# Two hybrid mixers: the pre-norm's token scale moved behind the first units, two norms merged into one stage, and filler matmuls dropped at the merged norms

## The reference, cut to what matters

```python
def second_block(x, ...):                    # x is _rmsnorm(h, final_norm) of the first block
    for l in range(DEPTH):                   # DEPTH = 2
        h = rms_norm(x, norm_mix_pre[l])
        mix = hybrid_mixer(h, w_in[l], ...)  # h @ w_in, h @ w_gate, four branches, w_out
        x = x + rms_norm(mix, norm_mix_post[l])
        h = rms_norm(x, norm_ffn_pre[l])
        x = x + rms_norm(swiglu(h, w_ffn_in[l], w_ffn_out[l]), norm_ffn_post[l])
    return x
```

## Time and profile before

| | us |
|---|---|
| median of 3 runs (lowest to highest) | 3116.38 (3113.12 to 3118.59) |
| the profiled execution, its own time | 3116.57 |
| its span in the profile | 3114.8 |
| PE busy | 3023.1 (97%) |
| PE weight loads busy | 2644.7 (85%) |
| DVE busy | 1688.2 (54%) |
| ACT busy | 1341.7 (43%) |

### The profile page before, as it was taken

The page is one execution under the profiler, slowest core; times in us unless marked ns, Lnnn a source line. Parts: engine busy times, 40 slices in busy tenths (PEclk is TensorE's granted clock), DMA queues, the critical chain, the costliest instruction groups (busy, mean ns, idle before and its releaser), DMA issues.

```text
span 3114.8 us, 52232 instructions
## 1 busy us (share of the span) xinstructions
PE 3023.1 (97%) x20192; PEld 2644.7 (85%) x20192; DVE 1688.2 (54%) x2641; ACT 1341.7 (43%) x1953; POOL 0.2 (0%) x4
## 2 busy tenths in 40 slices
PE   6999999989999999999998999999999999999999
PEld 4777778877777878888888999999899999998998
DVE  4333354545333353334666566677766666776666
ACT  3322233424322343323335655555654545556544
POOL 0000000000000000000000000000000000000000
PEclk9999999999999999999999998999999999999999
DMA  8656453115566233332322655455456544554564
GB/s 266 178 172 189 144 173 98 55 35 156 160 190 191 83 96 102 91 101 81 121 83 85 181 172 162 127 158 161 131 149 188 170 132 141 163 156 135 156 180 131
DMA packets 639022, 439.41 MB, mean 141 GB/s; under 512 B 22180, under 2 KB 627200, under 8 KB 638720
## 3 DMA queue, kind: packets, MB, share of 16 engines
q1 hardware_dynamic: 638848, 436.93, 47.5%
HBM read 430.84 MB, written 1.05 MB: 139 GB/s over the span
## 4 chain that ended last, share of the span: by engine, by line
PE 89%; DVE 7%; ACT 2%; issue 1%; DMA 1%; SPq 1%; ACTq 0%; DVEq 0%
PE ps L446 27%; PE ps L447 26%; PE ps L448 26%; PE ps L526 2%; DVE wlo L395 2%; PE ps L841 1%; ACT whi L389 1%; DVE normed L2326 1%; PE ps L1601 1%; PE ps L1569 1%; DVE xl L2318 1%; PE ps L1589 1%; DMA mod_w<-ada_w 0%; PE ps L868 0%; DVE h_gates L3043 0%
## 5 line engine op out<-in xcount | busy, mean ns | idle before, releaser
L446 PE MATMUL ps<-xh,whi 128*128 128x256 f32 (+1 forms) x3744 | 1221.7, 326 | 19.8 <-DVE wlo L395 5.2
L447 PE MATMUL ps<-xl,whi 128*128 128x256 f32 (+1 forms) x3744 | 1199.5, 320 | 0.0
L448 PE MATMUL ps<-xh,wlo 128*128 128x256 f32 (+1 forms) x3744 | 1198.5, 320 | 0.0
L395 DVE TENSOR_TENSOR wlo<-raw,whi 128x1024 fp32r<-128x1024 f32 x732 | 867.9, 1221 | 197.5 <-ACT whi L389 191.8
L389 ACT ACTIVATE whi<-raw 128x1024 fp32r<-128x1024 f32 x732 | 747.4, 1052 | 477.9 <-PE ps L448 432.5
L446 PEld LDWEIGHTS ps<-xh,whi 128*128 128x128 f32 x3744 | 715.7, 191 | 112.8 <-issue 32.8
L448 PEld LDWEIGHTS ps<-xh,wlo 128*128 128x128 f32 x3744 | 715.7, 191 | 51.3
L447 PEld LDWEIGHTS ps<-xl,whi 128*128 128x128 f32 x3744 | 716.5, 191 | 47.9
L446 PE MATMUL ps<-hid_h,whi 128*128 128x512 f32 (+1 forms) x1056 | 358.2, 339 | 0.2 <-DVE wlo L395 0.2
L447 PE MATMUL ps<-hid_l,whi 128*128 128x512 f32 (+1 forms) x1056 | 355.5, 337 | 0.0
L448 PE MATMUL ps<-hid_h,wlo 128*128 128x512 f32 (+1 forms) x1056 | 355.0, 336 | 0.0
(11 more groups left out here) (361 smaller groups left out, 2660.3 us busy)
## 6 DMA issues: line engine op xcount, KB each, us to landing
raw<-ffn_w_in SPq DMA_DIRECT2D x176, 512.0 KB, 4.8
mod_w<-ada_w SPq DMA_DIRECT2D x72, 1024.0 KB, 5.2
raw<-w_in SPq DMA_DIRECT2D x96, 512.0 KB, 4.5
raw<-w_ffn_in SPq DMA_DIRECT2D x88, 512.0 KB, 4.7
raw<-w_gate SPq DMA_DIRECT2D x64, 512.0 KB, 4.2
raw<-ffn_w_out SPq DMA_DIRECT2D x64, 384.0 KB, 4.0
raw<-ffn_w_out SPq DMA_DIRECT2D x64, 320.0 KB, 3.7
raw<-w_branch SPq DMA_DIRECT2D x32, 512.0 KB, 3.5
```

What stands on the lines that cost most here:

```text
L395: nc.vector.tensor_tensor(wlo[:, s, h, :], raw[:, s, h, :], whi[:, s, h, :].bitcast(F32), ALU.subtract).then_inc(S("lo_ready"), 1)
L446: nc.tensor.matmul(dst, w_h, x_h, start=start, stop=False)
L447: nc.tensor.matmul(dst, w_h, x_l, start=False, stop=False)
L448: return nc.tensor.matmul(dst, w_l, x_h, start=False, stop=stop)
```

## The change

The two norms in front of each mixer become one stage `merge`, as in front of the feed-forward networks. The mixer's first two units (`among_first`, `among_second`) take the one-column sums and the spread between their matmuls. All six units read unscaled chunks, and DVE multiplies by `tok_scale` where it empties their banks, in place of the copy. The other products of the mixer need scaled chunks: beside units 3 and 4, DVE and ACT make them in the second half of `xh`/`xl` (`second_pieces`, `second_highs`), and the small product and `beside_block` read them there. In layer 0 `merge` writes `hT` directly and adds nothing. At all four merged norms the two filler matmuls ahead of the spread and the three behind it are dropped. The last norm (`renorm` before `store`) keeps its form.

```diff
@@ pe_blocks @@
-                for j, b in sorted(order) if x_ready else order:
+                if x_ready:
+                    order.sort()
+                for j, b in order:
...
-                m.then_inc(S("mm_done"), 1)
+                    if (j, b) == order[-1]:
+                        m.then_inc(S("mm_done"), 1)
+                    if among:
+                        among(k, b)
@@ schedule @@
-        schedule += [("renorm", hT, lambda k: V("final_norm", k), True)]
+        post, by_post = lambda k: V("final_norm", k), False
...
-                ("norm", hT, 1, None, gain("norm_mix_pre_2")),
-                ("mamba", layer, w_in),
+                ("merge", hT if layer == 0 else h_out, post, gain("norm_mix_pre_2"), by_post),
+                ("mamba", layer, w_in, gain("norm_mix_pre_2")),
...
-                ("renorm", h_out, gain("norm_ffn_post_2"), layer == 0, True),
             ]
-        schedule += [("store",)]
+            post, by_post = gain("norm_ffn_post_2"), True
+        schedule += [("renorm", h_out, post, False, by_post), ("store",)]
@@ tensor: beside_block @@
-                        m = three(dst, w_h[:, k % 4, cols], w_l[:, k % 4, cols], xh[:, k, 0:T], xl[:, k, 0:T],
+                        m = three(dst, w_h[:, k % 4, cols], w_l[:, k % 4, cols], xh[:, k, T:2 * T], xl[:, k, T:2 * T],
@@ tensor: mamba @@
+                def among_first(k, b):
+
+                    if b == 1 and k:
+                        renormed_sum(k - 1)
+                    if (k, b) == (DC - 1, 1):
+                        renormed_sum(k)
+
+                def among_second(k, b):
+
+                    if (k, b) == (2, 0):
+                        spread_rstd(NT, 0)
+
+                pe.wait_ge(S("root_ready"), c.of["norm"])
@@ tensor: stages @@
                 elif stage == "merge":
-                    spread_rstd(NT)
+                    spread_rstd(NT, 0)
                     c.add(renorm=DC)
                     x_ready = norm_ready(1)
-                    warm(3, 3)
@@ scalar: mamba @@
-                pairs_of(act, c, 3, lambda i, s: None, ahead=past_odd(act_split, 1), first=True)
+                def second_highs(i, s):
+
+                    if (i, s) == (0, 0):
+                        token_scale()
+                    for k in range(4 * s, 4 * s + 4) if i == 1 else ():
+                        act.wait_ge(S("norm_prod"), c.of["norm_prod"] + k + 1)
+                        nc.scalar.activation(xh[:, k, T:2 * T], normed[:, k, 0:T], ACT.Copy).then_inc(S("norm_hi"), 1)
+                pairs_of(act, c, 3, second_highs, ahead=past_first(act_split), unroll=True)
@@ vector: merge @@
+                added = src is not hT
...
-                    if 1 <= k <= DC:
+                    if added and 1 <= k <= DC:
@@ vector: mamba @@
+                def second_pieces(k0):
+
+                    for k in range(k0, k0 + 4):
+                        nc.vector.scalar_tensor_tensor(out=normed[:, k, 0:T], in0=hT[:, k, 0:T], scalar=gain(k),
+                                                       in1=tok_scale, op0=ALU.mult, op1=ALU.mult).then_inc(S("norm_prod"), 1)
+                    for k in range(k0, k0 + 4):
+                        dve.wait_ge(S("norm_hi"), c.of["norm_hi"] + k + 1)
+                        nc.vector.tensor_tensor(xl[:, k, T:2 * T], normed[:, k, 0:T], xh[:, k, T:2 * T].bitcast(F32),
+                                                ALU.subtract).then_inc(S("norm_lo"), 1)
...
-                    fm_evac(m_in, 0, T)(dve, c, i, s)
-                pairs_of(dve, c, 3, evacuate, ahead=past_odd(dve_split, 1), unroll=True)
+                    if (i, s) == (0, 0):
+                        token_scale()
+                    if i == 1:
+                        second_pieces(4 * s)
+                    unit_done(dve, c, i, s)
+                    u = 2 * i + s
+                    nc.vector.tensor_tensor(m_in[:, 2 * u:2 * u + 2, :], ps[:, 2 * s:2 * s + 2, 0:T],
+                                            tok_scale.unsqueeze(1).to_broadcast([P, 2, T]), ALU.mult)\
+                        .then_inc(S("evac_done"), 1)
+                    if (i, s) == (0, 0):
+                        dve_split(dve, 0, 0, c.units + 2)
+                pairs_of(dve, c, 3, evacuate, ahead=past_first(dve_split), unroll=True)
```

More of the change, by code:

```diff
@@ L859, in ss_sum @@
                 m.then_inc(S("ss_mm"), 1)
[L861 to L871, removed]
             def renormed_sum(k):
@@ L1451, in mamba @@
                 beside = Beside(0, MAMBA_PLACES)
+                def among_first(k, b):
[7 more added lines that the diff above has]
+                pe.wait_ge(S("root_ready"), c.of["norm"])
                 pairs_of(pe, c, 3, lambda i, s: pe_blocks(pe, c, i, s, DC, T, xh, xl, 2, 256,
-                                                          x_ready if is_first(i, s) else None), first=True)
+                                                          x_ready if is_first(i, s) else None,
+                                                          (among_first, among_second)[s] if isinstance(i, int) and i == 0 else None),
+                         first=True)
+                norm_ready(1)(DC - 1)
                 pe.wait_ge(S("m_sw_lo"), layer + 1)
                 for t in range(NT):
-                    tt = slice(t * P, (t + 1) * P)
+                    tt = slice(T + t * P, T + (t + 1) * P)
                     for k in range(DC):
@@ L1738, in post_root, with merge @@
                 ins.then_inc(S("root_ready"), 1)
-            def merge(gain):
-                root_of_sums(NT)
+            def merge(gain, by_post):
+                post_root() if by_post else root_of_sums(NT)
                 act_split(act, 0, 1, c.units + 1)
@@ L2335, in norm, with merge @@
                 return lambda: products(DC, DC * nc_)
-            def merge(src, post_gain, gain):
+            def merge(src, post_gain, gain, by_post):
+                added = src is not hT
                 rstd_of_root(NT)
@@ L2341, in merge @@
                     if k < DC:
-                        nc.vector.scalar_tensor_tensor(out=normed[:, k, 0:T], in0=src[:, k, 0:T], scalar=post_gain(k),
-                                                       in1=ps[:, 5, 0:T], op0=ALU.mult, op1=ALU.mult)\
-                            .then_inc(S("post_normed"), 1)
-                    if 1 <= k <= DC:
+                        dst = normed if added else hT
+                        ins = nc.vector.scalar_tensor_tensor(out=dst[:, k, 0:T], in0=src[:, k, 0:T], scalar=post_gain(k),
+                                                             in1=ps[:, 5, 0:T], op0=ALU.mult, op1=ALU.mult)
+                        ins.then_inc(S("post_normed" if added else "renormed"), 1)
+                    if added and 1 <= k <= DC:
                         dve.wait_ge(S("post_normed"), c.of["post"] + k)
@@ L2353, in merge @@
                                                        op1=ALU.subtract).then_inc(S("norm_lo"), 1)
-                c.add(norm=1, renorm=DC, post=DC, norm_hi=DC)
+                c.add(norm=1, renorm=DC, post=DC * added, norm_hi=DC)
                 dve_split(dve, 0, 1, c.units + 1, (0,))
@@ L2775, in turn, with mamba @@
                 nc.vector.tensor_tensor(x, x, xs, ALU.add).then_inc(S("a_turned"), 1)
-            def mamba(layer):
+            def mamba(layer, gain):
+                def second_pieces(k0):
[6 more added lines that the diff above has]
+                                                ALU.subtract).then_inc(S("norm_lo"), 1)
                 def small_low():
```

18 lines of the change are left out of this document (10 added, 8 removed).

## The result

The changed kernel takes **3126.84 us** (median of 12 executions, 3116.46 to 3139.30) against 3116.66 us for the kernel before (12 executions beside them, 3113.12 to 3118.59). The ratio is **1.0036**, 95% interval 1.0024 to 1.0049: slower, by more than the 0.2% that counted as no change. The executions themselves spread four times as far as those of before, 23 us in place of 5.5 (24 executions of before beside the experiments spread over 9 to 10 us). The profiled one, 3119.58 us with a span of 3117.8, lies near the low end.

What follows compares the result with a forecast made beforehand. PE, busy 97% of the span, was taken as the bound: 3116.6 less 13.1 us for merging plus 24.2 us for the clock falling without filler gives 3127.7, say 3128 us, slower; 8-in-10 range 3103 to 3136, the forecast's own 3122 to 3137.

Steps and rivals of the forecast that it cites:

- The merging: Two norms made one ahead of each mixer: gain 6.5 us in mixer 0 and 6.6 us in mixer 1, 13.1 us together.
- Emptying and scaled chunks: DVE's scaled emptying (0.7 us) and extra chunk work in the mixers stay hidden behind PE: cost 0, at most 2 us.
- It falls at all, or nearly all, of the four: Without filler, PE's clock drops to 0.50 at all, or nearly all, of the four merged norms.
- Rival 1: The clock holds at the merged norms without filler: 3103.5 us, faster; chance 0.22 together with the late-DVE case.
- The short price: At a merged norm, the clock is back after 3.3 us of dense work, costing 1.4 us.
- The long price: At a merged norm, the clock stays low through the first unit and into the second, costing 7.6 us.
- Three long and one short: Over the four merged norms, three long low-clock stretches and one short: 3 x 7.6 + 1.4 = 24.2 us.
- rival 2: Clock falls, but first units' own matmuls raise it: 3109 us all short, 3121.5 with two long; chance 0.33.
- Rival 2's rule: Activity releases the throttle, so first units' matmuls restore the clock: all four norms short, 4 x 1.4 = 5.6 us.

Runs made afterwards that it cites:

- e1: Changed kernel with two filler matmuls ahead of the spread and three behind it put back at all four merged norms; 3104.75 us, ratio 0.9951 to before.
- e8: Changed kernel with filler at all four norms, VectorE emptying each of the first five units of both mixers twice; 3103.31 us, ratio 0.9963 to before.
- e7: Changed kernel with only the three filler matmuls behind each merged spread put back, none ahead; 3105.28 us, ratio 0.9965 to before.
- e10: Changed kernel again, unaltered, traced for a third look at the clock; one execution, 3125.34 us.
- first trace: The changed kernel's own first profiled execution, unaltered; 3119.58 us.
- e9: Changed kernel again, unaltered, traced for a second look at the clock; one execution, 3122.30 us.
- e6: Changed kernel with only the two filler matmuls ahead of each merged spread put back, none behind; 3114.56 us, ratio 1.0003 to before.
- e3: Changed kernel with filler put back only at the two merged norms ahead of the feed-forward networks; 3117.51 us, ratio 0.9994 to before.
- e11: Changed kernel with only the two filler matmuls ahead of each merged spread, repeated unaltered for a second trace; one execution, 3113.92 us.
- e4: Changed kernel, no filler, one-column sums moved behind the first unit's products at all four merged norms; 3120.73 us, ratio 1.0007 to before.
- e5: Changed kernel with one-column sums behind the first unit's products and filler put back at all four merged norms; 3113.08 us, ratio 0.9991 to before.

## Why the prediction was right, and where it was not

The number (3128 against 3126.84) and the sign were right. The steps were right in kind, and two of them were off in size, in opposite directions; that the number came within 2 us is luck.

- **The merging: right to a few tenths.** From the spread to the second unit e1 takes 1905.58 - 1893.84 = 11.74 us in mixer 0 and 2504.36 - 2491.51 = 12.85 us in mixer 1, before 18.76 and 19.80. Less 0.50 us by which the second unit, with the spread in it, is longer (6.26 in place of 5.76; taken: 0.4), that is 6.5 and 6.45 us; the sum had 6.5 and 6.6. The first units take 9.28 us (1896.30 to 1905.58) and 9.62; the sum had 9.3 and 9.61. From mixer 0's spread to the last, e8 is 1215.23 - 1202.13 = 13.1 us shorter than before, the sum's 13.1. (e1 and e7 are 16.6 shorter there. The other 3.5 us lie between mixer 0 and FFN 0, where e8 and before show two more stretches at 0.50, 10.2 us together.) 3103.5 us was forecast with the clock held; e1, e7 and e8 gave 3104.75, 3105.28 and 3103.31.
- **Emptying and scaled chunks: right.** In the changed kernel's timeline of DVE the scaled emptying takes 0.69 us (taken: 0.7), starts 1905.85 - 1903.64 = 2.2 us into the second unit, and the split behind it ends 5.2 us into it; the sum had 2.2 and 5.3. From the emptying of the second unit to that of the fourth are 2 x 5.80 us (1910.11 to 1921.71), where PE takes 5.76 per unit; DVE falls back by less than 0.1 us:

```profile
1905.85 0.69 DVE L2819 TENSOR_TENSOR m_in<-ps,ss 128x512 f32<-128x512 f32 x1 [0.32 <-ACT ss L1765]
1906.45 2.35 DVE L395 TENSOR_TENSOR wlo<-raw,whi 128x1024 fp32r<-128x1024 f32 x2
1910.11 0.69 DVE L2819 TENSOR_TENSOR m_in<-ps,ss 128x512 f32<-128x512 f32 x1 [1.30 <-PE ps L448]
...
1921.71 0.68 DVE L2819 TENSOR_TENSOR m_in<-ps,ss 128x512 f32<-128x512 f32 x1
```

- **"It falls at all, or nearly all, of the four": right,** 12 times out of 12 in three traces. Rival 1 (the clock holds) needed the filler; e1 is that rival, built.
- **The short price, 1.4 us:** 1.0 to 1.7 us in the table (14.55 - 12.89, 15.55 - 13.89, 15.00 - 14.01).
- **The long price, 7.6 us: too small.** The yardstick alone grows by 8.1 us (20.95 - 12.89) to 8.5 (22.35 - 13.89). Taken on to the next norm's spread it is 9.2 us in mixer 0 (e10 against e8), 10.3 in FFN 0 (first trace against e1), and 8.8 in mixer 1 (e10 against e8), where e8 has one short stretch more further on (2735.0 to 2738.4), worth some 1.4 us, so rather 10.2. Two terms were short. At low clock a step of the first unit takes 17.06 / 8 = 2.13 us, where I had 6 x 0.213 + 0.70 = 1.98: the first matmul behind a pair of sums holds the next one off for 0.36 us (2310.59 to 2310.95) and not 0.21, 1.2 us in eight steps. (At full clock it does so too, 1897.39 to 1897.59, 0.20 in place of 0.12. The 0.44 us that the sum took for a pair at full clock has that in it; the 0.70 at low clock, from sums in a row, has not.) And the second unit stays low for 6.1 us in place of the 3.3 that I gave it, another 2.8 x (1 - 0.12/0.213) = 1.2.
- **Three long and one short: wrong, and it made up for the price.** The traces had one, one and two long. At the measured prices three long and one short would be 3104.75 + 9.2 + 10.3 + 10.2 + 1.7 = 3136.2 us, and two of each some 3104.75 + 2 x 9.9 + 2 x 1.6 = 3127.8, near the median. So the median is most likely the mixed form of rival 2 (two long, forecast at 3121.5) with the long stretch at its measured price; that is an estimate, since no execution at the median was traced. The step that failed is the one that gave each norm its own fate, "mixer 0 has the shortest gap, so I let one of the four be short". In the six traces of kernels with no filler behind mixer 0's spread and with the sums among the products, mixer 0 was short three times (first trace, e9, e6) and long three times (e10, e3, e11): its fate is drawn anew in each execution, and goes with where the clock falls (table above). The spread of 23 us, which the trace of a single execution could not show, follows for the most part from it; some comes from low stretches elsewhere, as in e9 and in the kernel before.
- **Rival 2's rule.** FFN 0's row has PE busy for 16.97 of 17.00 us at 0.50, and e4's has it busy for 3.5 us at 0.99 with a fall right behind. The Trainium skill ("TensorE: Matmul & The Clock Gate", Part 1) says that "the default state is throttled, and activity releases the throttle". The traces agree with it where the products stand alone (e4's first units, back after 3.4 to 6.8 us). With one-column sums among them they agree at some norms (mixer 0 of the first trace, back after 3.4 us) and not at others (FFN 0), so the busy share of a profile did not tell here when the clock would be back. With all four short the time would have been some 3104.75 + 4 x 1.6 = 3111 us.

**Open.** Why the place of the fall should decide between a short and a long stretch, and what sets that place. That sums among the products are needed for a long one is not shown: e4 has no long one at four norms and no execution above 3126.57, but only one trace of it was read, and its falls lie where kernels with the sums among the products show no long one either. Nor is it settled why 1.84 us of idle time cost the clock in mixer 0 of e6 and 2.52 us in FFN 0 did not; that the place of the gap in time decides, and not its length alone, fits e6 and e11, but was only argued.

## What to carry to other kernels

An unused matmul in PE's idle time is not free to remove: five per norm, 2.6 us of PE in a stretch that waits for DVE anyway, were worth 22 us in 3105. Before you take such filler out, look at what follows the gap: with wide matmuls alone behind it the low stretch stayed short in the one trace (3.4 to 6.8 us, e4), with one-column matmuls among them it lasted for 20 us and more at 7 of 19 norms. Put the filler into the last and longest gap before the dense work (e7), and when a kernel's executions suddenly spread by 20 us, compare PEclk between two executions before you look for anything else.

## What the hardware showed that I had not expected

- PE at 97% busy tells nothing of its clock: the same 80 instructions took 9.5 us in one kernel and 17.0 in the other, both at a busy share of 98% or more.
- Behind a block of 32 one-column matmul records (3.69 us, PE busy throughout) the clock stood at 0.50: at three of four such blocks in e4, and with filler in place (e5) at the two of the mixers.
- A program that does the same work each time ran in anything from 3102 to 3132 us (e6), and two traced executions of it (3103 and 3114 us) have their low stretches in different places; with filler behind the spread five executions lie within 3.4 us (e7; with all filler, e1, five within 6.6).
- The cost of a thin matmul is not only its own: behind a pair of sums the first wide matmul holds the next off for 0.20 us in place of 0.12 at full clock, and for 0.36 in place of 0.21 at 0.50.
